# Mixers of a two-layer encoder: products with the values of two steps issued together, with a third set of buffers for turned probabilities

## What is computed

```python
def swa_sink_attention(q, k, v, sinks, t5_bias):          # layer 0, "a"
    ...
    scores = jnp.where(valid, scores + bias, NEG_INF)
    m = jnp.maximum(jnp.max(scores, axis=-1, keepdims=True), sink)
    p = jnp.exp(scores - m)
    probs = p / (jnp.sum(p, axis=-1, keepdims=True) + jnp.exp(sink - m))
    out = jnp.einsum('bckgqs,bcskd->bcqkgd', probs.astype(vb.dtype), vb)
...
def stick_breaking_attention(q, k, v):                     # layer 0, "b"
        ...
        w = jnp.where(causal, jnp.exp(jax.nn.log_sigmoid(z) + later), 0.0)
        return jnp.einsum('bhqs,bhsd->bhqd', w.astype(vh.dtype), vh)
...
def chunk_band_attention(q, k, v, rel_table):              # layer 1, "c"
        ...
        sc = jnp.einsum('bqhd,bshd->bhqs', qc, kc).astype(jnp.float32) * scale + bias
        sc = jnp.where(valid[None, None, None, :], sc, NEG_INF)
        p = jax.nn.softmax(sc, axis=-1)
        return jnp.einsum('bhqs,bshd->bqhd', p.astype(vc.dtype), vc)
```

## Time and profile before

| | |
|---|---|
| median of 3 runs | 2407.72 us (2407.71 to 2413.1) |
| profiled execution, own time | 2406.24 us |
| its span in the profile | 2404.5 us |
| PE busy | 2317.4 us, 96% of the span |
| VectorE, ScalarE, GpSimd busy | 75%, 57%, 11% |
| mean granted TensorE clock | 0.986 |

### The profile page before, as it was taken

The page is one execution under the profiler, slowest core; times in us unless marked ns, Lnnn a source line. Parts: engine busy times, 40 slices in busy tenths (PEclk is TensorE's granted clock), DMA queues, the critical chain, the costliest instruction groups (busy, mean ns, idle before and its releaser), DMA issues. The chain is left out here.

```text
span 2404.5 us, 34223 instructions
## 1 busy us (share of the span) xinstructions
PE 2317.4 (96%) x12932; PEld 1890.3 (79%) x12932; DVE 1792.7 (75%) x2538; ACT 1364.2 (57%) x1690; POOL 276.4 (11%) x243
## 2 busy tenths in 40 slices
PE   8999998999999999999899999998989999999997
PEld 6777887877888888886677777776878888888884
DVE  4565556678999999997555454557679999999996
ACT  3454446126777777775444444444047777777763
POOL 0000000002111111111500000000011121111104
PEclk9999999999999999999999999999999999999999
DMA  4110003328999999999311111104159999999986
GB/s 132 24 32 27 27 10 98 134 107 352 391 386 377 385 384 385 389 386 339 111 47 40 45 38 38 38 36 169 45 194 404 396 396 400 388 379 379 375 341 264
DMA packets 156078, 534.40 MB, mean 222 GB/s; under 512 B 40160, under 2 KB 80120, under 8 KB 106760
## 3 DMA queue, kind: packets, MB, share of 16 engines
q1 hardware_dynamic: 136784, 498.46, 54.7%
q0 software_dynamic: 18496, 33.60, 3.7%
q10 hardware_dynamic: 632, 0.10, 0.0%
HBM read 515.23 MB, written 50.41 MB: 235 GB/s over the span
## 5 line engine op out<-in xcount | busy, mean ns | idle before, releaser
L367 DVE TENSOR_TENSOR arena<-arena,arena 128x2048 fp32r<-128x2048 f32 (+1 forms) x458 | 955.8, 2116 | 65.3 <-ACT arena L1994 50.6
L1994 ACT CAST arena<-arena 128x2048 fp32r<-128x2048 f32 x384 | 716.4, 1918 | 150.2 <-PE psum L1713 116.4
L1713 PE MATMUL psum<-arena,arena 128*128 128x512 f32 x3072 | 734.6, 395 | 0.0
L1713 PEld LDWEIGHTS psum<-arena,arena 128*128 128x128 f32 x3072 | 570.1, 189 | 114.7 <-issue 0.4
L664 PE MATMUL psum<-arena,arena 128*128 128x512 f32 x2016 | 505.9, 401 | 4.6 <-DVE arena L367 4.5
L664 PEld LDWEIGHTS psum<-arena,arena 128*128 128x128 f32 x2016 | 369.5, 189 | 98.4 <-issue 11.4
L1724 PE MATMUL psum<-arena,arena 128*128 128x512 f32 x1536 | 359.6, 390 | 2.8 <-DVE arena L367 2.8
L1724 PEld LDWEIGHTS psum<-arena,arena 128*128 128x128 f32 x1536 | 288.0, 188 | 64.0 <-DVE arena L367 4.0
L367 DVE TENSOR_TENSOR arena<-psum,arena 128x512 fp32r<-128x512 f32 (+1 forms) x186 | 160.1, 870 | 105.7 <-ACT arena L792 55.3
L809 ACT ACTIVATE arena<-arena,arena 128x640 f32<-128x640 f32 (+4 forms) x192 | 120.0, 626 | 199.5 <-DVE arena L907 148.7
L1210 PE MATMUL psum<-arena,arena 128*128 128x512 f32 x768 | 189.3, 403 | 7.0 <-ACT arena L363 6.9
(11 more groups left out here) (194 smaller groups left out, 1663.6 us busy)
## 6 DMA issues: line engine op xcount, KB each, us to landing
arena<-in_moe_w_gate SPq DMA_DIRECT2D x128, 1024.0 KB, 8.6
arena<-in_moe_w_up SPq DMA_DIRECT2D x128, 1024.0 KB, 7.7
arena<-in_moe_w_down SPq DMA_DIRECT2D x128, 1024.0 KB, 7.0
arena<-expert_rows SPq DMA_DIRECT2D x32, 512.0 KB, 11.2
x_rows<-arena SPq DMA_DIRECT2D x24, 512.0 KB, 2.6
arena<-in_c_w_in SPq DMA_DIRECT2D x24, 512.0 KB, 4.1
arena<-x_rows SPq DMA_DIRECT2D x24, 512.0 KB, 7.5
arena<-in_x SPq DMA_DIRECT2D x16, 512.0 KB, 6.9
```

The source lines that it names most:

```text
L367: return eng.tensor_tensor(tile, src, high.bitcast(F32), ALU.subtract)
L1713: mm = pe.matmul(bank(o), cs[:, c * P:(c + 1) * P], ws[:, c * FF:(c + 1) * FF], start=(k == 0 and c == 0), stop=(k == 2 and c == CH - 1))
L1994: act.copy(w_hi[w][:, cols], self.raw[w][:, cols]).then_inc(hi_ready[w], 1)
```

## The change

For the steps below `deferred` (24 in layer 0: all but the last of the softmax pairs; 56 in layer 1) `apply` is no longer issued in each step for the one before. It is issued at the even steps, for the two steps before, at the end of the step. From `deferred` + 1 on the order is as before. Since turned probabilities now live longer, there is a third set of buffers: below `deferred` they are used in turn by threes (`turned_at`), then by twos, and `keep_turned` waits for the products of the step that used the same buffer last (`last_at`). In layer 0 the third set lies where pairs "b" later keep their sigmoids, in layer 1 in a place that is otherwise free and in the rows of the last output chunk.

```diff
--- before.py
+++ after.py
@@ -542,6 +542,7 @@
                 probs_t = [[pen(SEQ) for _ in range(2)] for _ in range(2)]
+                probs_t.append([place(WK + 56, width), place(WK + 57, width)])
                 left.append([pen(SEQ), place(AT_ROWS + 28, SEQ)])
@@ -558,6 +559,7 @@
                 probs_t = [[pen(width) for _ in range(2)] for _ in range(2)]
+                probs_t.append([place(WK + 8, width), place(AT_ROWS + 28, width)])
                 assert pen.kb <= WK + 89
@@ -593,6 +595,16 @@
+            deferred = TILES * ((n_soft if has_b else len(plan.pairs)) - 1)
+
+            def turned_at(s):
+
+                return (deferred - s) % 3 if s < deferred else s % 2
+
+            def last_at(s):
+
+                return max([o for o in range(max(s - 3, 0), s) if turned_at(o) == turned_at(s)], default=-1)
@@ -716,7 +728,7 @@
-                                           probs_t[s % 2][h][:, b * P:(b + 1) * P],
+                                           probs_t[turned_at(s)][h][:, b * P:(b + 1) * P],
                                            start=(b == 0), stop=(b == pair.blocks[t] - 1))
                     mm.then_inc(o_ready, 1)
@@ -748,7 +760,10 @@
                             turn(s, h, "high")
-                    if s > 0 and not ahead_of_high:
+                    if s > deferred and not ahead_of_high:
+                        apply(s - 1)
+                    if 0 < s <= deferred and s % 2 == 0:
+                        apply(s - 2)
                         apply(s - 1)
                 apply(plan.steps - 1)
@@ -757,8 +772,8 @@
                 eng.wait_ge(t_ready[h], plan.group[s][what] + 1)
-                need(eng, o_ready, s - 1)
-                copy(probs_t[s % 2][h][:, a:b], bank(B_TURN + h)[:, 0:b - a]).then_inc(t_copied[h], 1)
+                need(eng, o_ready, last_at(s) + 1)
+                copy(probs_t[turned_at(s)][h][:, a:b], bank(B_TURN + h)[:, 0:b - a]).then_inc(t_copied[h], 1)
```

## The result

The changed kernel takes 2414.61 us, median of 12 runs, against 2408.05 us for the kernel before in as many: ratio 1.0029, interval 1.0019 to 1.0038. It is 6.6 us slower where 5 us faster was forecast. Its profiled execution has a span of 2411.5 us, 7.0 more than before; 1.6 us of these lie ahead of the first scores (53.50 against 51.93 us), where nothing was changed.

A forecast was written before the change was run, and what follows sets the result against it. PE's queue was taken to bound both mixers. Savings of 4.20 us in layer 1 and 1.05 in layer 0, less 0.30 lost in steps 16 to 24, gave 4.95 us and 2402.8 us, range 2400 to 2405.5.

The forecast's parts named there:

- What a group costs: PE's product groups: 0.15 us a group plus 0.0546 us a matmul, so a merge saves 0.15 us.
- Turn to scores: New transition in odd steps: costs no more than turn to products, 0.99 against 1.00 us for eight transposes.
- Copies, buffers, `keep_y`: Copies into the third buffers and keep_y's wait for the odd step's products: cost 0.
- Does the shorter odd step uncover a wait?: Odd steps on PE: no, the next turn keeps 0.7 us of room in layer 1, 0.2 in layer 0.
- The sum: Both mixers: 4.20 us gained in layer 1, 1.05 gained and 0.30 lost in layer 0, 4.95 in all.
- Steps 16 to 24: Layer 0, pair 2: odd steps already wait for VectorE, so merges there lose 0.3 us together.
- Rival (c), the clock: Layer 0, 133 to 162 us: new PE holes lower the clock, 5.8 us slower, 2413.6 us; chance 0.07.
- Rival (a): Start of a step's products: the 0.15 us is its waits, so merges bring 0, 2408.0 us; chance 0.13.
- (b): Turn to scores is cheap in a running queue: merges bring up to 0.33 us, 2396.5 us; chance 0.10.
- (d): New buffers make copies wait, holding PE 0.3 us at each of 40 pairs: 2414.8 us; chance 0.03.

The follow-up runs named there:

- x3: Changed kernel, but projection halves in layer 0's softmax pairs alternate between two PSUM banks: 2410.42 us, ratio 1.0012 to the kernel before.
- x6: Changed kernel, but products go by twos only at every fourth step, so steps 2 and 6 of each pair go without: 2410.47 us, ratio 1.0013.
- x9: Changed kernel, but two projection banks and merges up to step 16 in layer 0, only tiles 1 and 2 merged in layer 1: 2405.30 us, ratio 0.9999.
- x7: Changed kernel, but layer 1 merges only up to step 48, so steps 55 and 56 are as before: 2413.12 us, ratio 1.0021.
- x11: Control: kernel before, but in layer 1 VectorE reads halves of the values ahead of the upper copies: 2407.25 us, ratio 1.0008.
- x2: Changed kernel, but products go by twos in layer 1 alone, layer 0 as in the kernel before: 2412.66 us, ratio 1.0014.
- x10: Changed kernel, but in layer 1 VectorE reads halves of the values ahead of the upper copies: 2410.15 us, ratio 1.0015.
- x5: Changed kernel's third buffers and waits, but products issued each step as in the kernel before: 2407.99 us, ratio 1.0003.

## Why the prediction was wrong

The step that failed is the one on whether the shorter odd step uncovers a wait; the steps around it were right, or right in kind. Point by point:

- **What a group costs: right.** Joint groups measured 1.02 us for 16 products, and where nothing waited a merge saved 0.14 to 0.18 us (x3, x6, x9). By 0.15 for the group and 0.0546 for a matmul, 16 products would take 1.02 and 40 products 2.33 us, and that is what they took.
- **Turn to scores: right.** 0.53 us behind four transposes and 0.97 behind eight, as turn to products.
- **Copies, buffers, `keep_y`: right**, by the run of the buffers alone and by the changed kernel's list of waits.
- **"Does the shorter odd step uncover a wait?": this step failed.** I looked at one wait of PE behind the place where products were taken out, the turn of s + 1, and found 0.7 and 0.2 us of room. PE meets another one sooner, the first matmul of a new half of a projection, which needs `proj_kept` and so the read-out of the half that ended just before turn. I had called the four groups of a step "without a hole": in the rows shown above, the last of them starts 75.29 - 75.14 = 0.15 us after its release. No row of before carries this wait, as a wait that is just met leaves no mark. It could be found only by listing what each group waits for and looking up when that was ready. The wait costs 0.49 us in six of the eight odd steps of pairs 0 and 1 of layer 0 and more in the other two, and in layer 1 0.15, 0.19 and 0.59 us a pair behind tiles 1, 5 and 7 (the last in six pairs; pair 7 has no projection). All merges were to hold there; they brought 2.2 us lost instead of 1.05 gained in layer 0 and 1.8 lost instead of 4.2 gained in layer 1.
- **The sum, as it came out.** Layer 0 +3.3 instead of -0.75; layer 1 +1.8 instead of -4.2, and 1.7 for the clock at step 56: 6.8 us, against 6.6 by the medians. The mixers of the two profiled executions differ by 2.1 + 3.5 = 5.6 us, as the kernel before had the lower granted clock in layer 0 (0.96 against 0.98).
- **Steps 16 to 24: right in kind, too small.** From scores 16 to scores 26, at a clock of 1.00, they lost 1.0 us with one bank and with two, where I had 0.3. In the changed kernel PE waits 0.58 to 0.68 us for VectorE's minimum at the scores behind four odd steps in a row. From scores 18 to 26 of x7 against x11, the intervals without products give back 0.5 us and those with two groups cost 1.2.
- **Rival (c), the clock: right in kind, in the wrong place.** I expected it in pair 2 of layer 0, on new holes in odd steps. There the changed kernel had 1.00 from 154 to 159 us, where before had 0.69. It came at step 56 of layer 1, in all four traces that merge there (the changed kernel, x2, x3, x10) and in none of the eight others. The prediction did not look at that step. The length of the wait does not tell the two apart: it was 1.85, 1.86, 1.85 and 1.31 us in the four and 1.51 or 1.52 in the eight. What differs in all is that 20 products had gone from ahead of it and stood behind it; why that brings the fall no run shows. Rival (a) is refuted by the joint groups (1.02 us), (b) by turn to scores in x3 and the changed kernel, (d) by x5 and the list of waits.
- **The chances.** The slower rivals (c) and (d) had 0.10 in mine, too little for a change that thins out the work in front of one wait after the other in a queue without slack. 2414.6 us lies above the range of 2397.5 to 2409.

## What to carry to other kernels

When work is taken out of a queue, list every wait of that queue behind the gap, up to the first that is late anyway, and for each look up when its release comes; a wait met with 0.15 us to spare looks in a timeline like none. Work that a step does "for nothing" may be the cover for a buffer with a single copy, so give that buffer a second copy first or move the work between steps in which no such buffer changes hands. Where the steps that lose work already wait for another engine, taking it out gives little back. A saving that is real on its own rows (0.15 us here) must be compared with what it uncovers (0.49 us), not with the engine's busy time, which fell by 3.4 us while the kernel became slower.

## What the runs showed of the hardware

- The product group of 128x64 form between groups of other forms costs 0.15 us beyond its matmuls, and one group of twice the size has that cost once: 1.02 us against 2 x 0.59.
- The clock of PE fell to the lower level at one place in one order of work and not in another, in every trace: four of four traces with the merge at step 56 fell, none of eight without it. There 40 products took 3.67 to 4.00 us behind waits of 1.31 to 1.86 us, and 2.33 at full clock.
- Falls elsewhere come and go between executions of about the same order: layer 0's mixer had a granted clock of 0.96 in the kernel before and 1.00 in x11, with 141.27 and 136.74 us. That is 4.5 us, as much as the change was to bring, and traces must be compared at equal clock before a stretch is read.
